# Output projection blocks: sixteen transposes in one piece, and token rounding ahead of weight units 5 and 6

## The reference

```python
merged = (g_ret * y_ret + g_att * y_att)
x = x + jnp.einsum('bsd,de->bse', merged, w_out[l])        # 2048 -> 2048
h2 = rms_norm(x, norm_ffn_g[l])
u = jnp.square(jax.nn.relu(jnp.einsum('bsd,df->bsf', h2, w_up[l])))   # 2048 -> 8192
x = x + jnp.einsum('bsf,fd->bsd', u, w_down[l])
return rms_norm(x, norm_final_g)
```

## Time and profile before

| | us |
|---|---|
| median of 3 runs | 1577.64 |
| lowest, highest | 1577.01, 1577.89 |
| the profiled execution: device time | 1577.22 |
| the profiled execution: span from the first to the last instruction | 1575.3 |
| TensorE matmul busy | 1563.6 (99%) |
| VectorE busy | 1023.6 (65%) |
| ScalarE busy | 794.8 (50%) |
| mean granted TensorE clock | 0.999 of full |

### The profile page before, as it was taken

One profiled execution on the slowest core, in us unless ns is written; L12 is line 12 of the kernel. 1 busy time (PEld: TensorE's weight loads), 2 busy tenths in 40 slices (PEclk: granted clock), 3 DMA queues, 4 the chain that ended last, 5 costly groups with the idle time before them and its releaser, 6 DMA issues.

```text
span 1575.3 us, 18861 instructions
## 1 busy us (share of the span) xinstructions
PE 1563.6 (99%) x6976; PEld 1284.2 (82%) x6976; DVE 1023.6 (65%) x1344; ACT 794.8 (50%) x1023; POOL 39.3 (2%) x52
## 2 busy tenths in 40 slices
PE   9999999999999999999999999999999999999998
PEld 7777777888888888888878888888888888888886
DVE  5977877544456777666699877337753676337744
ACT  6554555443444444444444555555555555555553
POOL 0000000000000000000000000000000000000000
PEclk9999999999999999999999999999999999999999
DMA  9644544556655564556565877888778887887873
GB/s 361 206 138 156 186 150 158 187 199 207 210 184 162 187 211 163 185 195 205 200 222 191 250 242 232 252 233 253 237 238 252 242 244 221 250 243 240 253 217 117
DMA packets 154392, 333.93 MB, mean 212 GB/s; under 512 B 5600, under 2 KB 5728, under 8 KB 149856
## 3 DMA queue, kind: packets, MB, share of 16 engines
q1 hardware_dynamic: 149296, 299.61, 55.5%
q0 software_dynamic: 4464, 32.51, 10.8%
q10 hardware_dynamic: 576, 1.06, 0.2%
HBM read 298.55 MB, written 2.10 MB: 191 GB/s over the span
## 4 chain that ended last, share of the span: by engine, by line
PE 94%; DVE 3%; issue 1%; DMA 0%; ACT 0%; SPq 0%; POOLq 0%; POOL 0%; DVEq 0%; ACTq 0%
PE acc L413 91%; DVE buf L973 1%; DVE wlo L964 1%; PE pps L453 1%; PE tps L428 1%; DMA raw<-in_w_in 0%; PE pps L438 0%; DVE qT L973 0%; ACT whi L645 0%; PE sps L446 0%; DVE ta_lo L1363 0%; PE tps L555 0%; PE tps L554 0%; PE tps L553 0%; DVE final L1375 0%
## 5 line engine op out<-in xcount | busy, mean ns | idle before, releaser
L645 ACT ACTIVATE whi<-raw 128x1024 fp32r<-128x1024 f32 x542 | 572.4, 1059 | 664.2 <-PE acc L413 660.2
L964 DVE TENSOR_TENSOR wlo<-raw,whi 128x1024 fp32r<-128x1024 f32 x480 | 585.9, 1225 | 461.8 <-ACT whi L645 458.7
L413 PE MATMUL acc<-whi,ta_hi 128*128 128x512 f32 x1308 | 517.4, 396 | 0.8 <-DVE ta_lo L1007 0.4
L413 PE MATMUL acc<-whi,ta_lo 128*128 128x512 f32 x1308 | 509.7, 390 | 0.0
L413 PE MATMUL acc<-wlo,ta_hi 128*128 128x512 f32 x1180 | 459.6, 389 | 0.0
L413 PEld LDWEIGHTS acc<-whi,ta_hi 128*128 128x128 f32 x1308 | 245.6, 188 | 56.5 <-issue 4.3
L413 PEld LDWEIGHTS acc<-whi,ta_lo 128*128 128x128 f32 x1308 | 245.5, 188 | 51.7
L413 PE MATMUL acc<-whi,tb_hi 128*128 128x512 f32 x736 | 287.3, 390 | 0.0
L413 PE MATMUL acc<-whi,tb_lo 128*128 128x512 f32 x736 | 286.5, 389 | 0.0
L413 PEld LDWEIGHTS acc<-wlo,ta_hi 128*128 128x128 f32 x1180 | 221.6, 188 | 47.4 <-issue 2.4
L413 PE MATMUL acc<-wlo,tb_hi 128*128 128x512 f32 x616 | 239.7, 389 | 0.0
(11 more groups left out here) (139 smaller groups left out, 797.7 us busy)
## 6 DMA issues: line engine op xcount, KB each, us to landing
raw<-in_w_in SPq DMA_DIRECT2D x66, 1024.0 KB, 5.1
raw<-in_w_up SPq DMA_DIRECT2D x64, 1024.0 KB, 5.4
raw<-in_w_down SPq DMA_DIRECT2D x64, 1024.0 KB, 5.2
raw<-in_w_gate SPq DMA_DIRECT2D x32, 1024.0 KB, 5.3
low<-raw POOLq DMA_DIRECT2D x31, 1024.0 KB, 8.1
raw<-in_w_att SPq DMA_DIRECT2D x16, 1024.0 KB, 5.0
raw<-in_w_ret SPq DMA_DIRECT2D x16, 1024.0 KB, 5.0
raw<-in_w_out SPq DMA_DIRECT2D x16, 1024.0 KB, 5.3
```

The source lines that it names most:

```text
L413: last = nc.tensor.matmul(acc[B.parity][:, t, :], a[:, k, tok], b, start=(k == 0 and n == 0), stop=(k == KCH - 1 and n == 2))
L645: nc.scalar.activation(whi[:, s:s + UCH, :], raw[:, u * UCH:(u + 1) * UCH, :], ACT.Copy).then_inc(hi_ready, 1)
L964: V_.tensor_tensor(wlo[:, s:s + UCH, :], raw[:, u * UCH:(u + 1) * UCH, :], whi[:, s:s + UCH, :].bitcast(f32), ALU.subtract).then_inc(lo_re ...
```

## The change

VectorE, blocks 33 to 37: all 16 transposes come in one piece (`turn_whole`), then, for j = 1 to 4, the gain; then unit 4 is rounded; then the low part of the activations is made; then units 5, 6 and 7 are rounded. ScalarE: the high part of the activations is made ahead of units 5 and 6 instead of between 6 and 7. No instruction is added or removed, and no size changes.

```diff
@@ ScalarE, for j in range(GROUPS + 1) @@
                 negated(B)
-                split(B, 5, 7)
                 if j == 0:
                     hi_from_turned(T_STAGE4 + 3, tc_hi, 3)
                 else:
                     hi_from_gained(T_STAGE5 + j - 1, buf[2], ta_hi, j - 1)
-                split(B, 7, 8)
+                split(B, 5, 8)
@@ VectorE, new helper @@
+            def turn_whole(before, src, ready, n):
+
+                dve.wait_ge(ready, n)
+                dve.wait_ge(t_free, before)
+                turn(by_chunk(src), to_tokens(turned), 0, len(pieces), t_full)
+
@@ VectorE, for j in range(GROUPS + 1) @@
                 if j == 0:
-                    split_and_turn(B, 4, 6, T_STAGE4 + 3, buf[3][:], m_ready, 4)
-                    split(B, 6, 7)
+                    turn_whole(T_STAGE4 + 3, buf[3][:], m_ready, 4)
+                    split(B, 4, 5)
                     lo_from_turned(8, tc_hi, tc_lo, 3)
+                    split(B, 5, 7)
                 else:
                     prev = Block(B5 + j - 1)
-                    split_and_turn(B, 4, 6, T_STAGE5 + j - 1, mix[:, :, (j - 1) * COLS:j * COLS],
-                                   evacuated[prev.parity], prev.turn + 1)
+                    turn_whole(T_STAGE5 + j - 1, mix[:, :, (j - 1) * COLS:j * COLS],
+                               evacuated[prev.parity], prev.turn + 1)
                     gain(T_STAGE5 + j - 1, buf[2], gffn, j - 1)
-                    split(B, 6, 7)
+                    split(B, 4, 5)
                     lo_from_gained(8 + j, buf[2], ta_hi, ta_lo, j - 1, h2T_ready)
+                    split(B, 5, 7)
                 split(B, 7, 8)
```

## The result

| | before | after |
|---|---|---|
| median, us | 1577.66 (4 runs) | 1591.05 (4 runs) |
| lowest, highest | 1577.01, 1577.89 | 1590.02, 1591.48 |
| profiled execution: device time, span | 1577.22, 1575.3 | 1590.02, 1588.1 |
| mean granted TensorE clock of that execution | 0.999 | 0.997 |

The ratio of after to before is 1.0085, with a 95% interval from 1.0073 to 1.0097. The change makes the kernel 13.4 us slower, which is clear of the noise. The forecast was 1588.5 with a range from 1587.0 to 1591.5.

The account below looks back on a forecast made before the run. TensorE, 94% of the chain of waits, was taken to bound the kernel. 2.70 + 10.36 - 1.24 - 0.74 = +11.08 us on 1577.22 gave 1588.30, by the median 1588.7; forecast 1588.5, range 1587.0 to 1591.5.

Parts of the forecast that it names:

- The stalls at unit 4: Blocks 33 to 37: TensorE waits for unit 4, losing 2.70 us in block 33 and 2.59 in each other.
- The two old stalls: Waits at unit 5 of block 33 and unit 6 of block 37 go, minus 1.24 and 0.74 us.
- Unit 5 in time: Blocks 33 to 37: unit 5 is ready before TensorE wants it, by 0.5 us in block 37; no cost.
- ScalarE's move free: Loop: ScalarE making the tokens' high part ahead of units 5 and 6 costs nothing.
- the loads free: SyncE's loads of units 4 and 5 come 2.3 us later, TensorE 2.6 us later too; no cost.
- The sum for the order: Blocks 33 to 37: new stalls less the two old ones, +11.08 us, giving 1588.30, or 1588.7 by the median.
- The clock: Rival: clock falls in the five new stalls, 13.6 us more, about 1602; chance 0.04.
- a unit 5 that would be late: Rival: a second stall in each of five blocks, at most 1.2 us each, +6, about 1594.5; chance 0.06.
- Nothing gained at the ends alone: Rival: only the loop's two ends gain; blocks 34 to 36 spared, 3 x 2.59 less, 1580.7; chance 0.02.
- the piece of sixteen did not get cheaper: Faster rival: block 33's sixteen transposes take 4.66 us instead of 7.22, unit 4 in time, 1575.2; chance 0.02.

Follow-up runs that it names:

- kernel with filled stalls: Changed kernel with ten matmuls of no use on TensorE ahead of its wait for unit 4 in blocks 33 to 37: 1588.50 us.
- the ends alone: Changed kernel with the new order kept only in blocks 33 and 37 and the old order in blocks 34 to 36: 1583.50 us.
- one piece alone: Kernel before with all sixteen transposes ahead of unit 4, the rest and ScalarE in the old order: 1585.40 us.
- the tokens first: Changed kernel with transposes again in two pieces of eight, unit 4 between them, token rounding still ahead of units 5 and 6: 1599.45 us.
- the last version: Kernel before with block 33's unit 5 rounded after 12 transposes and, in blocks 34 to 37, ScalarE applying the gain instead of VectorE: 1576.07 us.

## Why the prediction was right, and what it missed

**The stalls at unit 4: right, in place, number and size.** The prediction had 2.56 us of waiting and 0.14 of restart in block 33, and 2.45 and 0.14 in blocks 34 to 37, with blocks of 24.4 us. The trace has blocks of 24.46 and 24.32 to 24.34 us, and TensorE comes to unit 4 2.56 and 2.43 us late. The forecast of 13.06 us for the five stalls stands against 2.70 + 4 x 2.57 = 12.98.

**The two old stalls: right.** No wait at unit 5 of block 33, none on `ta_lo`. TensorE did wait 0.2 us for a `low4` transfer once in the whole run, in block 43, against none before. The second trace of the same changed kernel has no such wait, so it does not belong to the order; five of the other eight traces have one of 0.2 to 0.6 us, and why was not looked into.

**Unit 5 in time, ScalarE's move free, the loads free: right.** The half microsecond of slack for unit 5 held (896.66 against 897.16 in block 37). ScalarE's order put back changed nothing. Neither TensorE nor ScalarE waits for a load of weights in the loop.

**The sum for the order: right.** It gave 1588.3 by the profiled execution and 1588.7 by the median. The kernel with filled stalls, where the mean clock shows a fall in none of five runs, takes 1588.50.

**The clock: the step that failed.** The prediction argued that TensorE had stood for over 4 us at the end of the run before the clock fell, "and a stall of 2.3 should pass too", and gave the fall 0.04, all five at once for 13.6 us. The runs showed that a stall of 2.3 us passes in most cases and not in all, which is the sign of being wrong that the prediction itself had named ("if the clock drops behind a stall"). A fall costs 1.6 us in the changed kernel (7 or 8 slow matmuls), not the 2.72 of a whole slow unit, and its two traces have one and two falls, at a mean clock of 0.997 and 0.996; three of the four executions behind the median of 1591.05 have 0.996. Up to two falls are the 2.5 us between 1588.5 and 1591.05. That the median still lies in the range is in part luck: the sum had nothing for the clock, and the room above it, some 2 us, was set aside for a unit 5 that would be late and was not.

The single pause at the end of the trace was a poor witness: it shows how late the clock fell, not the shortest pause behind which it can. The delay is no tolerance. In the loop the ten falls of all traces began 2.0 to 4.5 us after the stall's start, and in eight of them TensorE was at work again by then. At the end of the ten traces the clock fell 2.1 to 4.7 us after the last matmul; the 4.4 us of the kernel before was one of the five longer delays. In the changed kernel's trace the last matmul is over at 1580.55, and the clock is down 2.4 us later:

```profile
1580.00:1581.00 1.00, 0.55 (x3) 0.13 (x1) 0.41 (x1) 0.00 (x0) 0.00 (x0) 1.00 0.00 0
...
1582.00:1583.00 1.00, 0.00 (x0) 0.00 (x0) 0.31 (x3) 0.03 (x1) 0.51 (x1) 1.00 0.00 0
1583.00:1584.00 1.00, 0.00 (x0) 0.00 (x0) 0.92 (x2) 0.92 (x1) 0.04 (x1) 0.50 0.00 0
```

The rival of the falling clock was the right one to fear. The Trainium skill, TensorE: Matmul & The Clock Gate, "Part 1: The HAM clock gate", says of the rise to full clock that its moment varies from run to run, since it depends on where in the chip's own timing the first matmul lands. The falls here vary too: the two traces of the changed kernel have one fall and two, and the one in block 36, which both have, begins 1.3 us after TensorE resumed in one and 1.5 us in the other. That the reason is the same was not tested.

**Sizes of the other rivals.** Nothing gained at the ends alone (1583.50), and the piece of sixteen did not get cheaper: 7.21 us to the next instruction's start (884.68 to 891.89), against 7.22 taken for it.

**The arithmetic of the range.** Its own terms give 1587.2 and 1591.3 rather than 1587.0 and 1591.5. Nothing hangs on it.

## What to carry to other kernels

Where one engine feeds the bound one from a list of steps, write down for each step when its result is wanted and when the list delivers it, both from the block's start. Work that is wanted a block later must not stand ahead of work wanted next, even if it is short and even if it removes a visible stall elsewhere. Price a new stall of TensorE above its length: if it is as long as those of 2.3 us here, a fall of the clock may come on top, some 1.6 us each here, and the test for it is to fill the stall with matmuls that nobody reads. How long the clock holds out in one long pause does not say how long a pause is safe.

## What the runs showed of the hardware that was not expected

The clock can fall behind a stall of 2.3 us, and where it falls varies. In the changed kernel it fell with TensorE at work again since 868.35, as the windows above show. With one piece alone it fell 0.3 us before TensorE resumed, and with the tokens first it had fallen in block 33 a microsecond before TensorE came back at 799.20:

```profile
797.00:798.00 1.00, 0.00 (x0) 0.00 (x0) 1.00 (x2) 1.00 (x2) 0.00 (x0) 1.00 0.00 0
798.00:799.00 1.00, 0.00 (x0) 0.00 (x0) 1.00 (x2) 1.00 (x2) 0.00 (x0) 0.50 0.00 0
```

A fall may thus lie wholly behind the stall that brought it, where no view of waits shows it: only the granted clock and the 0.43 us steps do. By the profiled executions, it fell behind none of the stalls of 0.4 to 1.1 us in this loop (two in the kernel before, four with one piece alone, one in the last version), behind 6 of the 18 of 2.3 to 2.4 us (1 of 5 and 2 of 5 in the changed kernel, 1 of 5 with ScalarE's old order, 1 of 2 with the ends alone, 1 of 1 with one piece alone), and behind 4 of the 5 of 3.2 us. These are few cases, and what decides a single one was not found. Nor does TensorE's restart behind a stall come from its standing still: in the filled kernel, too, the first real matmul lasts 0.50 us instead of 0.39, and its blocks are as long.
